# First stage's norms and casts re-ordered on their engine queues, the merge cut into five tiles of 410 columns, the last block finished by halves

## The chip, the cores and the metric

One Trainium2 chip; the same program runs on 8 cores with different data, without exchange between them. The time of a run is the device time of the slowest core, in microseconds (us). Engines: PE multiplies matrices, DVE and POOL work on vectors, ACT evaluates functions (and squares, scales, copies), SP issues most of the DMAs. Each engine works through its own queue in program order and waits there on semaphores.

## The reference, cut to what matters

```python
h = rmsnorm(x, norm_mix_pre)                     # x / rms(x) * w
q_m, k_m, v_m, i_m, f_m, o_m, q_f, k_f, v_f, f_f, g_a, g_b = split(h @ w_in)
h_a = mlstm_chunkwise(q_m, k_m, v_m, log_i, log_f)      # 4 heads, matrix memory
h_a = rmsnorm(h_a, ml_head_norm) * sigmoid(o_m)
y_a = h_a @ w_branch_a
h_b = forgetting_attention(q_f, k_f, v_f, log_fg)       # 8 heads, causal softmax
y_b = h_b @ w_branch_b
merged = sigmoid(g_a + b_gate_a) * y_a + sigmoid(g_b + b_gate_b) * y_b
x = x + rmsnorm(merged @ w_out, norm_mix_post)
h = rmsnorm(x, norm_ffn_pre)
a, g = split(causal_dwconv(h @ w_up, conv_w, conv_b))
x = x + rmsnorm((gelu(g) * a) @ w_down, norm_ffn_post)
```

x is (4, 4096, 1024); two cores share a batch row, each computes 2048 output tokens.

## The kernel before, in words

A core sees 32 blocks of 128 tokens. Blocks 0 to 14 (and 8 of them for the other half of the row) are only read for state and keys; blocks 15 to 31, 17 in number, are its own (block 15 gives a halo of two tokens). Nothing schedules the program: the Python code appends operations to five queues, a dependency tracker turns reads and writes of named buffers into semaphore waits, and each queue runs in the order in which it was written.

**Stage B (the mLSTM, 0 to about 412 us).** Each block of x is loaded, squared and summed on ACT (`A_sq`), turned into 1/rms (`rms_rstd`: a small multiply-add on DVE, then a power on POOL), scaled to bf16 on DVE (`A_sc`), transposed on PE and copied from PSUM on DVE (`A_T`). Blocks 0 to 7 are done first, in a lead-in loop that also runs the K projection of a block (`K_proj`, evacuated on ACT) and the gate columns (`A_G`). Every eight blocks the gates go through `gates_slot` (DVE add, ACT tanh), `gates_slot_b` (DVE, ACT exp), `gates_slot_c` (ACT ln, DVE negate into LF) and `gates_slot2` (two PE matmuls of LF, then small ACT and DVE work). Then one step for each chunk `c` in the order MSEQ (0 to 14, 16 to 23, 15, 24 to 31), `cn` being the next one: projections of `cn` (`QK_proj` of up to four blocks when `cn` opens a tile, `V_proj` in two halves, `O_proj` in two halves), state update `upd`, output `num_mm`, its norm (`num_post`: four ACT squares, small DVE work, a POOL power) and product (`num_fin` on DVE), and the store of the result `hablk` to memory (`T_ha`, on SP). `ctb` scales the state to bf16 on ACT for the next `num_mm`; `state_step` mixes states at three places. The projections take two PSUM banks in turn, so a projection waits until the one before the last is evacuated by ACT. `hablk` and the banks of `num_mm` are each reused: `hablk` every second chunk, and before this change `num_post` wrote its unused squares into `hablk` too. Weights arrive in f32 in twelve pieces and are cast to bf16 by `W_cast`, the last six at fixed places in `A_sc`, on POOL. From step 15 on, every step also issues one 1 MB conversion of `w_up` from POOL's queue (`conv_job`), whose DMA shares the 16 DMA engines with the stores.

**Stage C (attention, to about 966 us)** is not touched. **Stage D1, the merge (966 to 1194 us):** for each of 8 output column chunks and each token tile, four groups of 8 matmuls into four PSUM banks, two sigmoids on ACT, two products on DVE, a sum on POOL into `mergedT`. The tiles are 2 columns (the halo) and four times 512. The weights of the next chunk are cast (`wd_cast`: POOL and DVE) during the chunk. **Stage D2 and E** are the output projection and the FFN, in four tiles of four blocks; at the end of a tile each block's down projection is squared on ACT, normed, added (POOL) and stored.

```python
        def rms_rstd(col, inv_n):      # dve tensor_scalar, then pool pow
        def A_sq(b):                   # act Square + rms_rstd(b)
        def A_sc(b):                   # dve scale; W_cast(LOAD_AT[b - 4]); W_load; A_load
        def num_post(c):               # 4 act squares, dve, pool pow
        def num_fin(c, p):             # dve: hablk = bank * scale * gate
```

## Time and profile before

| | us |
|---|---|
| median of 3 runs | 1733.96 (1731.91 to 1738.88) |
| the profiled execution | 1734.73 |
| its span, slowest core (4) | 1733.2 |
| spans of all cores | 1714.6 (core 7) to 1733.2 |
| PE busy on core 4 | 1637.2 (94%) |

The span is measured from the first to the last instruction of a core; the time has 1.5 us more around it. All sums below are made on core 4's trace. In the timelines a row has the start, the duration (of several merged instructions, from the first start to the last end), engine, line, operation, shapes and count, and in brackets how long the engine stood idle before and what ended the wait. Matmuls are pipelined, so a single one shows a latency that is longer than its share of a series.

### The profile page before, as it was taken

The page shows a single profiled execution, that of the slowest core. Times are in us where ns is not written, and L with a number is a line of the kernel's source. Part 1 is how long each engine was busy: PE and PEld are TensorE (multiplying, and loading weights), DVE is VectorE, ACT ScalarE, POOL GpSimd, SP SyncE. Part 2 cuts the span into 40 slices and gives each one's busy share as a digit, 9 for nine tenths or more (in the row PEclk, how much of TensorE's full clock was granted, in tenths as well). Part 3 has the DMA queues.
Part 4 walks back from the last instruction along what each step waited for, and adds up shares of the span by engine and source line. Part 5 has one row for each costly group of instructions (what it writes and reads, how often), then busy time and mean ns, then how long its engine had stood idle before and what let it go on. Part 6 is the DMA issues. An engine that isn't in the chain of part 4 may idle for free.

```text
span 1733.2 us, 36312 instructions; the slowest of 8 cores (1714.6 to 1733.2 us)
## 1 busy us (share of the span) xinstructions
PE 1637.2 (94%) x12448; PEld 915.4 (53%) x12448; DVE 833.5 (48%) x1599; ACT 904.9 (52%) x1709; POOL 447.6 (26%) x564
## 2 busy tenths in 40 slices
PE   3789996999999999999998999999999999999997
PEld 2345543455776776776775444444454444444443
DVE  4574644455334334333343223232887387584781
ACT  3455654555477677677678422122665164362551
POOL 1031111101111111111112223232843343343442
PEclk9899998999999999999999999999999999999999
DMA  9261368533632231331222522215684353443421
GB/s 296 94 222 62 68 82 119 69 56 62 102 37 27 30 40 23 32 48 23 32 35 59 113 89 69 78 50 155 180 252 138 76 183 95 136 161 81 146 98 49
DMA packets 102083, 163.23 MB, mean 94 GB/s; under 512 B 72848, under 2 KB 75152, under 8 KB 92688
## 3 DMA queue, kind: packets, MB, share of 16 engines
q1 hardware_dynamic: 78432, 134.50, 26.6%
q0 software_dynamic: 23040, 25.69, 12.9%
q8 instruction: 104, 1.70, 0.4%
q10 hardware_dynamic: 432, 0.72, 0.2%
q14 instruction: 75, 0.61, 0.1%
HBM read 160.63 MB, written 30.15 MB: 110 GB/s over the span
## 4 chain that ended last, share of the span: by engine, by line
PE 81%; DVE 5%; ACT 5%; issue 3%; DMA 3%; POOL 2%; SPq 0%; DVEq 0%; POOLq 0%; ACTq 0%
PE psum L381 51%; PE psum L1084 10%; PE psum L1638 6%; PE psum L1228 6%; PE psum L1561 5%; ACT arena L1208 2%; DVE arena L520 1%; ACT arena L528 1%; DMA ha_scr<-arena 1%; DMA arena<-x 1%; DMA arena<-wup_scr 1%; PE psum L505 1%; POOL arena L1665 1%; DVE arena L1419 1%; PE psum L818 1%
## 5 line engine op out<-in xcount | busy, mean ns | idle before, releaser
L381 PE MATMUL psum<-arena 128*128 128x512 bf16 (+2 forms) x6796 | 1138.2, 313 | 39.8 <-ACT arena L528 16.5
L381 PEld LDWEIGHTS psum<-arena 128*128 128x128 bf16 x6796 | 548.2, 99 | 490.6 <-issue 74.2
L1208 ACT ACTIVATE arena<-psum,arena 128x512 bf16<-128x512 f32 (+1 forms) x576 | 370.9, 651 | 144.4 <-PE psum L381 132.1
L1594 DVE SCALAR_TENSOR_TENSOR arena<-psum,arena 128x511 f32<-128x511 f32 x352 | 255.1, 746 | 48.5 <-POOL arena L1583 19.6
L1061 DVE CAST arena<-psum 128x512 bf16<-128x512 f32 (+3 forms) x164 | 104.2, 642 | 246.9 <-PE psum L1084 133.5
L1084 PE MATMUL psum<-arena 128*128 128x512 bf16 (+3 forms) x896 | 219.2, 348 | 3.5 <-DVE arena L1061 2.6
L1228 PE MATMUL psum<-arena 128*128 128x129 bf16 x2112 | 214.0, 220 | 1.5 <-POOL arena L1213 1.2
L1228 PEld LDWEIGHTS psum<-arena 128*128 128x128 bf16 x2112 | 155.3, 98 | 70.2 <-issue 2.8
L1638 PE MATMUL psum<-arena 128*128 128x512 bf16 x704 | 153.1, 379 | 1.5 <-POOL arena L1609 1.3
L1577 ACT ACTIVATE arena<-psum,arena 128x512 f32<-128x512 f32 x176 | 135.6, 778 | 23.2 <-PE psum L381 20.9
L1213 POOL TENSOR_TENSOR arena<-arena 128x128 bf16<-128x128 bf16 x128 | 59.1, 469 | 336.6 <-ACT arena L1208 334.9
L1609 POOL TENSOR_TENSOR arena<-arena 128x512 bf16<-128x512 f32 x88 | 112.9, 1283 | 110.1 <-ACT arena L1606 97.8
L351 POOL TENSOR_TENSOR arena<-arena 128x1 f32<-128x1 f32 x82 | 50.4, 620 | 278.1 <-DVE arena L348 278.1
L1638 PEld LDWEIGHTS psum<-arena 128*128 128x128 bf16 x704 | 68.6, 98 | 85.2 <-issue 2.9
L520 DVE SCALAR_TENSOR_TENSOR arena<-arena,psum 128x256 f32<-128x256 f32 (+1 forms) x188 | 81.2, 476 | 64.9 <-PE psum L1228 46.1
L1084 PEld LDWEIGHTS psum<-arena 128*128 128x128 bf16 x896 | 80.2, 98 | 56.6 <-issue 6.7
L1357 ACT ACTIVATE arena<-psum,arena 128x512 f32<-128x512 f32 (+1 forms) x40 | 24.0, 601 | 140.2 <-PE psum L381 140.1
L528 ACT ACTIVATE arena<-psum 128x512 bf16<-128x512 f32 (+3 forms) x93 | 51.3, 556 | 84.2 <-PE psum L381 83.8
L1363 DVE TENSOR_TENSOR arena<-psum,arena 128x512 f32<-128x512 f32 (+1 forms) x40 | 23.4, 585 | 133.9 <-ACT arena L1357 118.1
L528 ACT ACTIVATE arena<-psum,arena 128x256 bf16<-128x256 f32 x128 | 53.3, 467 | 60.9 <-PE psum L381 60.4
L1561 PE MATMUL psum<-arena 128*128 128x512 bf16 x352 | 85.0, 376 | 0.0
L1369 POOL TENSOR_TENSOR arena<-arena 128x512 bf16<-128x512 f32 (+1 forms) x40 | 44.3, 1107 | 155.9 <-DVE arena L1366 155.8
(114 smaller groups left out, 1222.8 us busy)
## 6 DMA issues: line engine op xcount, KB each, us to landing
arena<-wup_scr SPq DMA_DIRECT2D x44, 1024.0 KB, 5.8
arena<-x SPq DMA_DIRECT2D x33, 512.0 KB, 5.9
arena<-w_merge SPq DMA_DIRECT2D x32, 512.0 KB, 6.2
arena<-w_mem SPq DMA_DIRECT2D x12, 1024.0 KB, 10.9
wup_scr<-w_up POOLq DMA_DIRECT2D x11, 1024.0 KB, 15.1
arena<-x SPq DMA_DIRECT2D x8, 1024.0 KB, 8.0
out<-arena SPq DMA_DIRECT2D x16, 512.0 KB, 2.9
arena<-w_fox POOLq DMA_DIRECT2D x24, 256.0 KB, 4.8
```

Source lines behind the costliest of these rows:

```text
L381: ins = e.matmul(out_ap, lhsT=l, rhs=r, start=(i == 0), stop=(i == n - 1))
L520: pg.add("dve", lambda e: e.scalar_tensor_tensor(out=o, in0=a, scalar=sc_, in1=b_, op0=op0, op1=op1), reads=rd, writes=wr)
L528: pg.add("act", lambda e: e.activation(out=o, in_=a, func=func, scale=scale, bias=bias), reads=rd, writes=wr)
L1061: pg.add("dve", lambda e: e.tensor_copy(out=out_ap, in_=in_ap), reads=rd, writes=wr)
L1084: ins = e.matmul(bank(bk)[:, 0:w_], lhsT=Wqk.ap[:, kc, which * P:(which + 1) * P], rhs=tv[:, kc, :], start=(kc == 0), stop=(kc == KC - 1))
L1208: pg.add("act", lambda e: e.activation(out=pt.ap[:, c0:512], in_=bank(lgb)[:, 0:512 - c0], func=AF.Exp, scale=float(P) ** -0.5, bias=bias_ ...
L1228: ins = e.matmul(bank(ACC[tl % 2][i // 2])[:, (i % 2) * 129:(i % 2) * 129 + 129], lhsT=pt.ap[:, i * P:(i + 1) * P], rhs=vx[s_].ap[:, j, :] ...
L1561: e.matmul(bank(bk)[:, 0:w_], lhsT=l, rhs=r, start=(kc == 0), stop=(kc == KC - 1))
L1577: pg.add("act", lambda e, ups=ups, yb=yb, cidx=cidx, ag=ag, w_=w_: e.activation(out=yb.ap[:, ag, 0:w_], in_=ups[:, 0:w_], func=AF.Identity ...
L1594: pg.add("dve", lambda e, ups=ups, yb=yb, cidx=cidx, sh=sh, jw=jw, ag=ag, w_=w_: e.scalar_tensor_tensor(out=yb.ap[:, ag, sh:w_], in0=ups[: ...
L1609: pg.add("pool", lambda e, yb=yb, gl=gl, fi=fi, w_=w_: e.tensor_tensor(out=actb.ap[:, fi, 0:w_], in0=gl.ap[:, 0:w_], in1=yb.ap[:, 0, 0:w_] ...
L1638: ins = e.matmul(bank(bs[hh]), lhsT=actb.ap[:, fc, bl * P:(bl + 1) * P], rhs=Wdn(fc)[:, hh * 512:(hh + 1) * 512], start=(fc == 0), stop=(f ...
```

## The change

Six things. (1) `rms_rstd` leaves `A_sq`: it is queued, and emitted by `A_rstd`, at fixed places or at the latest in front of the `A_sc` that needs it. (2) The twelve weight casts alternate between ACT and DVE, none is on POOL; the loads of the last six, and so their casts, come earlier. (3) In the lead-in the K projection runs one block earlier, and the casts 2 to 5 are moved. (4) In the chunk loop `gates_slot_c` comes right behind `num_mm`, `ctb` and `state_step` go behind the second V projection, and `gates_slot2` behind the first O projection (for own chunks); `num_post` writes its unused squares into the scratch `jk`. (5) The merge runs in five tiles of 410 columns that begin at the halo's two columns. (6) The last block of the last tile is squared, scaled, added and stored in two halves of 512 columns, the first sum on POOL, the second on DVE.

```diff
         PIECES = [(ch, hf) for ch in (1, 2, 3, 0, 4, 5) for hf in range(2)]
-        CAST_ENG = ("act", "dve", "act", "dve", "pool", "dve") + ("pool",) * 6
-        LOAD_AT = {b: j for j, b in enumerate(range(12, 18), 6)}
+        CAST_ENG = ("act", "dve") * 6
+        LOAD_AT = {b: j for j, b in enumerate((10, 12, 14, 16, 17, 19), 6)}
...
+        sqq = []
         def A_sq(b):
...
-            rms_rstd(b, 1.0 / D)
+            sqq.append(b)
+
+        def A_rstd():
+            while sqq:
+                rms_rstd(sqq.pop(0), 1.0 / D)
         def A_sc(b):
...
+            if b in sqq:
+                A_rstd()
...
             def num_post(c):
-                hb_, gw = hablk[par], Gw[par]
+                gw = Gw[par]
                 for h in range(4):
                     pg.add("act", lambda e, h=h: e.activation(
-                        out=hb_.ap[:, h * 256:(h + 1) * 256], in_=bank(RB[h // 2])[:, h % 2 * 256:h % 2 * 256 + 256],
+                        out=jk.ap[:, h * 256:(h + 1) * 256], in_=bank(RB[h // 2])[:, h % 2 * 256:h % 2 * 256 + 256],
                         func=AF.Square, scale=eb_t.ap[:, c, h:h + 1], accum_out=sc.ap[:, par, 0, h:h + 1]),
-                        reads=[bank_u[RB[h // 2]], (eb_t.u, c // 8)], writes=[(sc.u, (par, "q")), (hb_.u, h)])
+                        reads=[bank_u[RB[h // 2]], (eb_t.u, c // 8)], writes=[(sc.u, (par, "q")), (jk.u, h)])
...
             A_sq(1)
             A_sc(1)
             A_sq(2)
+            pg.add("dve", lambda e: e.tensor_copy(out=Wg.ap, in_=Wgf.ap), reads=[Wgf], writes=[Wg])
+            K_proj(0)
             A_T(1)
-            pg.add("dve", lambda e: e.tensor_copy(out=Wg.ap, in_=Wgf.ap), reads=[Wgf], writes=[Wg])
+            A_G(0)
             for b in range(2, 8):
                 A_sc(b)
                 if b < 7:
                     A_sq(b + 1)
                 A_T(b)
-                K_proj(b - 2)
-                A_G(b - 2)
-            W_cast(2)
-            A_G(6)
+                if b < 7:
+                    K_proj(b - 1)
+                A_G(b - 1)
+                if b == 6:
+                    W_cast(2)
             A_G(7)
             gates_slot(0)
+            W_cast(3)
             gates_slot_b()
-            W_cast(3)
             gates_slot_c()
+            W_cast(5)
             W_cast(4)
             for b in range(8, 12):
                 A_load(b)
             gates_slot2(0, SB1)
             V_proj(0, 0)
-            W_cast(5)
             V_proj(1, 0)
             A_sq(8)
             A_sc(8)
                 if own(c):
                     gs = G_all()
                     num_mm(c)
+                    if late is not None:
+                        gates_slot_c()
                     if fresh or not own(cn):
...
                         gates_slot_c()
+                    A_rstd()
...
                     k_trans(cn)
                     if own(c) and not fresh:
                         num_post(c)
+                    A_rstd()
                 if cn is not None and (own(cn) or cn > 5):
                     V_proj(cn, 0)
                 if own(c) and cn is not None:
                     upd(c, 0)
                     upd(c, 1)
-                    if cn in (15, 24):
-                        state_step(cn)
-                    elif own(cn):
-                        ctb(cn, 0)
-                        ctb(cn, 1)
                 if own(c):
                     num_fin(c, 0)
                     num_fin(c, 1)
-                if late is not None and own(c):
-                    gates_slot_c()
                 if gs is not None:
                     gates_slot(gs)
                 if tails:
                     A_T(tails[0])
                 if cn is not None:
                     V_proj(cn, 1)
-                if late is not None:
-                    gates_slot2(late, TB if own(cn) else SB1)
+                if own(c) and cn is not None:
+                    if cn in (15, 24):
+                        state_step(cn)
+                    elif own(cn):
+                        ctb(cn, 0)
+                        ctb(cn, 1)
+                if late is not None and not own(cn):
+                    gates_slot2(late, SB1)
                 if gs is not None:
                     gates_slot_b()
                 gs2 = gs
...
                 if own(cn):
                     O_proj(cn, 0)
+                if late is not None and own(cn):
+                    gates_slot2(late, TB)
...
+            MT0, MTW = P - 2, 410
             for cc in range(KC):
                 wd = Wd[cc % 2]
                 wd_load(cc + 1)
-                for (eb0, nb_) in EXT_TILES:
-                    w_ = nb_ * P if eb0 else 2
-                    t0 = eb0 * P if eb0 else P - 2
+                for dt in range(5):
+                    t0, w_ = MT0 + dt * MTW, MTW
                     bs = [0, 1, 2, 3] if dstep % 2 == 0 else [4, 5, 6, 7]
                     dstep += 1
                     srcs = (haT, hbT, xnT_own, xnT_own)
...
                         if src is xnT_own:
-                            rd = [(src.u, NPRE + eb0 + j) for j in range(nb_)]
+                            rd = [(src.u, NPRE + j) for j in range(t0 // P, (t0 + w_ - 1) // P + 1)]
                         elif src is haT:
                             rd = [haT]
                         else:
-                            rd = [(src.u, (h, eb0 if eb0 else "E")) for h in range(8)]
+                            rd = [(src.u, (h, e0 if e0 else "E")) for h in range(8) for (e0, n0) in EXT_TILES
+                                  if e0 * P < t0 + w_ and (e0 + n0) * P > t0]
...
-                    if eb0 == 9:
+                        reads=[m1, m2], writes=[(mergedT.u, (cc, dt))])
+                    if dt == 3:
                         wd_cast(cc + 1)
...
-                                 bank_u[p0 + hh], [(mergedT.u, (kc, tile_eb[eb])) for kc in range(KC)] + [(Wout.u, hh)])
+                                 bank_u[p0 + hh], [(mergedT.u, (kc, dt)) for kc in range(KC) for dt in range(5)
+                                  if MT0 + dt * MTW < (eb + 1) * P and MT0 + (dt + 1) * MTW > eb * P] + [(Wout.u, hh)])
...
+                    elif last and ib == 3:
+                        for hh in range(2):
+                            e3_mm(bl, hh, bs, 0, NFC)
+                            pg.add("act", lambda e, hh=hh, bs=bs, tme=tme: e.activation(
+                                out=tme.ap[:, hh * 512:hh * 512 + 512], in_=bank(bs[hh]), func=AF.Square,
+                                accum_out=ssq.ap[:, 90 + hh:91 + hh]),
+                                reads=[bank_u[bs[hh]]], writes=[(ssq.u, 90 + hh), (tme.u, hh)])
+                        tt(ssq.ap[:, 90:91], ssq.ap[:, 90:91], ssq.ap[:, 91:92], ALU.add, [(ssq.u, 90), (ssq.u, 91)], [(ssq.u, 90)])
+                        rms_rstd(90, 1.0 / D)
+                        for hh, eng_ in ((0, "pool"), (1, "dve")):
+                            sl, xk = slice(hh * 512, hh * 512 + 512), (x1.u, eb) if hh else (x1.u, (eb, 0))
+                            stt(tme.ap[:, sl], bank(bs[hh]), rstd.ap[:, 90:91], wfpost_bc.ap[:, sl], ALU.mult, ALU.mult,
+                                [bank_u[bs[hh]], (rstd.u, 90), wfpost_bc], [(tme.u, hh)])
+                            pg.add(eng_, lambda e, eb=eb, tme=tme, sl=sl: e.tensor_tensor(
+                                out=x1.ap[:, eb, sl], in0=x1.ap[:, eb, sl], in1=tme.ap[:, sl], op=ALU.add),
+                                reads=[(tme.u, hh), xk], writes=[xk])
+                            pg.add("sp", lambda e, eb=eb, sl=sl: e.dma_start(out=out_d[(eb - 1) * P:eb * P, sl], in_=x1.ap[:, eb, sl]),
+                                   reads=[xk], writes=[(out_u, "o%d_%d" % (eb, hh))], dma="outh%d" % hh)
+                        continue
...
```

How the order on two queues moves. DVE in the lead-in, from the scaling of block 2 (SCALAR_TENSOR_TENSOR 128x1024 is `A_sc`, TENSOR_SCALAR 128x1 the DVE half of `rms_rstd`, COPY the one in `A_T`), before:

```order
L486 SCALAR_TENSOR_TENSOR arena<-arena 128x1024
L348 TENSOR_SCALAR arena<-arena 128x1
L508 COPY arena<-psum 128x8x128
L486 SCALAR_TENSOR_TENSOR arena<-arena 128x1024
L348 TENSOR_SCALAR arena<-arena 128x1
```

and now:

```order
L494 SCALAR_TENSOR_TENSOR arena<-arena 128x1024
L516 COPY arena<-psum 128x8x128
L348 TENSOR_SCALAR arena<-arena 128x1
L494 SCALAR_TENSOR_TENSOR arena<-arena 128x1024
L516 COPY arena<-psum 128x8x128
```

The norm's DVE half went from in front of the copy to behind it, directly in front of the scaling that needs its result.

ACT in the steps of chunks 22 and 23 (128x256 from psum,arena is half a V projection's evacuation or, at L780/L788, a square of `num_post`; 128x256 from arena is `ctb`; 128x64 is tanh, the 128x96 are exp and then ln of the gates; 128x512 is an O projection's tanh; 128x128 x8 evacuates the Q and K of block 15), before:

```order
L780 ACTIVATE arena<-psum,arena 128x256 x4
L528 ACTIVATE arena<-psum,arena 128x256 x2
L528 ACTIVATE arena<-arena 128x256 x4
L528 ACTIVATE arena<-arena 128x64
L528 ACTIVATE arena<-psum,arena 128x256 x2
L528 ACTIVATE arena<-arena 128x96
L528 ACTIVATE arena<-psum 128x512 x2
L780 ACTIVATE arena<-psum,arena 128x256 x4
L528 ACTIVATE arena<-psum 128x128 x8
L528 ACTIVATE arena<-psum,arena 128x256 x2
L528 ACTIVATE arena<-arena 128x256 x4
L528 ACTIVATE arena<-arena 128x96
```

and now:

```order
L788 ACTIVATE arena<-psum,arena 128x256 x4
L536 ACTIVATE arena<-psum,arena 128x256 x2
L536 ACTIVATE arena<-arena 128x64
L536 ACTIVATE arena<-psum,arena 128x256 x2
L536 ACTIVATE arena<-arena 128x256 x4
L536 ACTIVATE arena<-arena 128x96
L536 ACTIVATE arena<-psum 128x512 x2
L536 ACTIVATE arena<-arena 128x96
L788 ACTIVATE arena<-psum,arena 128x256 x4
L536 ACTIVATE arena<-psum 128x128 x8
L536 ACTIVATE arena<-psum,arena 128x256 x4
L536 ACTIVATE arena<-arena 128x256 x4
```

`ctb` went behind the second V evacuation, and the gates' ln in front of the squares.

PE between the second V projection of block 15 and its `num_mm` (128x96 are the two LF matmuls of `gates_slot2`, the 128x512 a V projection and then two O projections, or V and O and then O), before:

```order
L381 MATMUL psum<-arena 128x512 x8
L381 MATMUL psum<-arena 128x96 x2
L381 MATMUL psum<-arena 128x512 x16
L761 MATMUL psum<-arena 128x256
L762 MATMUL psum<-arena 128x256
```

and now:

```order
L381 MATMUL psum<-arena 128x512 x16
L381 MATMUL psum<-arena 128x96 x2
L381 MATMUL psum<-arena 128x512 x8
L769 MATMUL psum<-arena 128x256
L770 MATMUL psum<-arena 128x256
```

One O projection now stands in front of the LF matmuls.

## Rows read from the trace of the kernel before

**Rows 1.** The page: span, and busy time of the engines.

```profile
span 1733.2 us, 36312 instructions; the slowest of 8 cores (1714.6 to 1733.2 us)
...
PE 1637.2 (94%) x12448; PEld 915.4 (53%) x12448; DVE 833.5 (48%) x1599; ACT 904.9 (52%) x1709; POOL 447.6 (26%) x564
```

**Rows 2.** Timeline, lead-in: start, us, engine line operation [idle before <-what ended it].

```profile
35.38 1.28 DVE L486 SCALAR_TENSOR_TENSOR arena<-arena 128x1024 bf16<-128x1024 f32 x1 [0.63 <-POOL arena L351]
...
36.81 0.61 PE L505 MATMUL psum<-arena 128*128 128x128 bf16 x8 [1.01 <-DVE arena L486]
...
37.46 0.15 DVE L348 TENSOR_SCALAR arena<-arena 128x1 f32<-128x1 f32 x1 [0.79 <-ACT arena L478]
...
37.56 0.69 DVE L508 COPY arena<-psum 128x1024 bf16<-128x1024 bf16 x1
...
38.48 1.28 DVE L486 SCALAR_TENSOR_TENSOR arena<-arena 128x1024 bf16<-128x1024 f32 x1 [0.22 <-POOL arena L351]
...
42.00 2.75 DVE L486 SCALAR_TENSOR_TENSOR arena<-arena 128x1024 bf16<-128x1024 f32 x1 [0.22 <-POOL arena L351]
...
47.82 1.90 ACT L465 ACTIVATE arena<-arena 128x2048 bf16<-128x2048 f32 x1
...
52.73 7.52 PE L381 MATMUL psum<-arena 128*128 128x96 f32 x24 [4.91 <-DVE arena L524]
```

**Rows 3.** Timeline of core 4, chunks 19 and 22.

```profile
222.77 0.47 ACT L780 ACTIVATE arena<-psum,arena 128x256 bf16<-128x256 f32 x1 [4.04 <-PE psum L381]
...
225.93 11.97 PE L381 MATMUL psum<-arena 128*128 128x512 bf16 x51 [3.17 <-ACT arena L528]
...
267.69 1.89 PE L381 MATMUL psum<-arena 128*128 128x512 bf16 x8
...
272.35 0.47 ACT L780 ACTIVATE arena<-psum,arena 128x256 bf16<-128x256 f32 x1 [5.52 <-DMA ha_scr<-arena]
...
275.76 3.02 PE L381 MATMUL psum<-arena 128*128 128x512 bf16 x8 [3.91 <-ACT arena L528]
...
280.79 3.57 PE L381 MATMUL psum<-arena 128*128 128x512 bf16 x8 [2.01 <-ACT arena L528]
```

**Rows 4.** DMA issues, 250 to 256 us: line, queue, count, KB, us to landing.

```profile
ha_scr<-arena SPq DMA_DIRECT2D x1, 256.0 KB, 17.2
```

**Rows 5.** Timeline of core 4: QK_proj(16), the LF matmuls, O_proj(24).

```profile
168.99 10.52 PE L381 MATMUL psum<-arena 128*128 128x512 bf16 x48 [1.87 <-ACT arena L528]
...
302.56 6.32 PE L381 MATMUL psum<-arena 128*128 128x96 f32 x20 [6.10 <-DVE arena L524]
...
332.98 1.89 PE L381 MATMUL psum<-arena 128*128 128x512 bf16 x8 [2.21 <-ACT arena L528]
```

**Rows 6.** Timeline of core 7: QK_proj(16) and the LF matmuls.

```profile
164.46 10.52 PE L381 MATMUL psum<-arena 128*128 128x512 bf16 x48 [1.87 <-ACT arena L528]
...
286.14 5.77 PE L381 MATMUL psum<-arena 128*128 128x96 f32 x20 [6.10 <-DVE arena L524]
```

**Rows 7.** Timeline of core 4, before the LF matmuls: ACT.

```profile
298.80 1.71 ACT L528 ACTIVATE arena<-arena 128x256 bf16<-128x256 f32 x4 [3.67 <-DVE arena L517]
...
300.52 1.28 ACT L528 ACT_TABLE_LOAD   x1
```

**Rows 8.** Windows of PE over the merge: from:to, length, busy (count), clock, DMA, GB/s.

```profile
966.37:1194.50 228.13, 227.77 (x1280) 1.00 0.31 79
```

**Rows 9.** Timeline: POOL in the merge.

```profile
990.10 1.58 POOL L1369 TENSOR_TENSOR arena<-arena 128x512 bf16<-128x512 f32 x1 [5.64 <-DVE arena L1366]
...
991.64 2.34 POOL L1291 TENSOR_TENSOR arena<-arena 128x1024 bf16<-128x1024 f32 x1
```

**Rows 10.** Timeline, the end of the program.

```profile
1715.80 8.15 PE L1638 MATMUL psum<-arena 128*128 128x512 bf16 x37
...
1724.16 1.02 ACT L1658 ACTIVATE arena<-psum 128x1024 f32<-128x1024 f32 x1 [8.38 <-PE psum L1638]
...
1727.75 2.34 POOL L1665 TENSOR_TENSOR arena<-arena 128x1024 f32<-128x1024 f32 x1 [1.53 <-DVE arena L1662]
```

More of the change, by code:

```diff
@@ L1370, in build_program @@
                         out=mergedT.ap[:, cc, t0:t0 + w_], in0=m1.ap[:, 0:w_], in1=m2.ap[:, 0:w_], op=ALU.add),
-                        reads=[m1, m2], writes=[(mergedT.u, (cc, eb0))])
-                    if eb0 == 9:
+                        reads=[m1, m2], writes=[(mergedT.u, (cc, dt))])
+                    if dt == 3:
                         wd_cast(cc + 1)
@@ L1432, in build_program @@
                 load_group(k_)
-            tile_eb = {}
-            for (eb0, nb_) in EXT_TILES:
-                for j in range(nb_):
-                    tile_eb[eb0 + j] = eb0
             for n in range(NEXT + 3):
```

## The prediction, made before the change was run

> **What bounds the kernel now.** I read the page first. PE is busy 94% of the span [rows 1], so only two things can shorten the run: fewer PE cycles, or less waiting of PE. The windows by stage then showed that almost all of PE's idle time lies before 340 us, in stage B; the merge is full, so there only fewer cycles help. The waits of PE led to the timeline of stage B, where four kinds of wait stand out.
> The lead-in [rows 2]: a scaling (35.38), transposes (36.81), a copy (37.56), the next scaling (38.48), 3.1 to 3.5 us a block. One scaling took 2.75 us instead of 1.28, because a cast ran on POOL beside it, and PE then stood 4.91 us before the first LF matmuls at 52.73.
> Chunks 19 and 22 [rows 3]: ACT stands 4.04 and 5.52 us before the squares of `num_post`. The second is put down to the store `ha_scr`; that store took 17.2 us to land [rows 4], and 272.35 less 17.2 is its issue, about 255.1. The first is put down to PE, which had long been done; the square writes the same buffer that the store reads, so I take it for the same wait. Behind the squares stands the evacuation of a V projection, and PE waits 3.17, 3.91 and 2.01 us for it. After the waits eight matmuls take 3.02 and 3.57 us instead of the 1.89 at 267.69: PE is then for a while at the lower of its two levels (1.2 instead of 2.4 GHz), so a wait costs more than its own length.
> A check inside this trace: core 7 has none of these store waits, and its span is the 1714.6 us of [rows 1]. From the first Q/K projection (168.99 and 164.46) to the LF matmuls of the last eight blocks (302.56 and 286.14) core 4 needs 133.6 us and core 7 121.7 [rows 5, 6].
> Last, the LF matmuls at 302.56, with 6.10 us of idle PE on both cores [rows 5, 6].
>
> **The change, term by term** (core 4's trace; the profiled execution took 1734.7 us, 0.8 above the median of the runs).
>
> *Lead-in: -1.4.* The norm's DVE half now stands behind the copy, so the chain of a block is serial: 1.43 (scaling to transposes) + 0.75 (to the copy) + 0.69 - 0.1 (overlap) + 1.02 (norm half at 37.46 to the scaling at 38.48) = 3.8 us against 3.3 before, five times: +2.5. The POOL cast beside block 7 is gone: 2.75 - 1.28 = -1.5. The ACT cast of 1.90 at 47.82, which stood in front of the tanh, has moved into the loop, where ACT idles: -1.9. The last K projection no longer stands in front of the last gate matmuls (1.7 us, from eight matmuls in 1.89), but a DVE cast now does in front of `gates_slot_b` (1.2): -0.5. Ends: -4 (the chain hides behind PE) and +2.5 (only the chain shows).
>
> *Chunk loop, blocks 8 to 23: 0.* The six casts leave POOL for ACT (1.90 each, [rows 2]) and DVE. On DVE a scaling and a cast (about 2.5 us) take the place of a scaling of 2.8 that a POOL cast slows. Where a step has two new blocks, the norm half adds up to 1.0 us to DVE's chain. ACT has room beside PE. Both signs: -3 to +3. `A_rstd` in the other steps stands where its result is needed a projection later: nothing.
>
> *Squares into jk: -11.9.* They no longer wait for a store. I take the difference of the two cores, 133.6 - 121.7. What then remains is what core 7 has. `num_fin` still overwrites the stored buffer, but a good 5 us later in the step (about 17.5 us after the store's issue against 12.3), and 17.2 was the slowest store. POOL's queue also issues one 1 MB conversion earlier, in a stretch in which the DMA engines idled. Ends: -13 and -5.
>
> *Chunk 23 to block 24's Q and K: -1.8.* E is the end of chunk 23's last O projection, 280.79 + 3.57 = 284.36. Before: LF matmuls at E + 18.2, `num_mm(15)` at E + 24.5 (302.56 + 6.32), the third Q/K group of block 24 at about E + 29.0 (1.0 for num_mm and two groups of 1.73). Now `num_mm(15)` waits for `ctb` alone: it began at E + 14.4 [rows 7]; ln and its table load come in front of the squares (+1.5), `num_fin` in front of `state_step` (+1.7), so it ends at 14.4 + 3.2 + 1.7 = E + 19.3. But ACT then has everything in a row: table load 1.28, two tanh and the gate operations (about 3.2, sized from 1.71 for the four operations of 256 columns of `ctb`), squares and first evacuation (3.4, from 272.35 to 275.76): third group at E + 27.2. So 5 us come free, and 3.4 are given back to ACT's queue. Ends: -6 and +2.
> The table load took 1.28 us in this trace, and started 0.01 us after the work before it (298.80 + 1.71 = 300.51, [rows 7]). The Trainium skill (ScalarE: Activation LUTs, What ACT_TABLE_LOAD costs) adds a drain and gives about 2.66 us for every switch of a set. With that the two loads on this path would cost some 2.8 us more and the term would be +1.0; the row shows no such gap, so the sum goes by the row.
>
> *State step of block 24: -0.7.* PE waited 2.21 us for a V evacuation that stood behind `ctb` [rows 5]. The evacuation is now in front, but the next `num_mm` waits for a `ctb` that is 1.7 later.
>
> *The merge: -5.9.* Eight matmuls of 512 columns took 1.89 us [rows 3], eight of 128 columns 0.61 [rows 2]: 1.28 / 8 / 384 = 0.417 ns a column. 48 of 512 columns took 10.52 [rows 5], so one more costs (10.52 - 1.89) / 40 = 215.8 ns, and one of 410 columns 215.8 - 102 x 0.417 = 173.3. Before: 1024 of 512 columns and 256 of two, 228.1 in all and 227.8 of them busy [rows 8], which leaves about 28 ns for a two-column one. Now 1280 x 173.3 + 0.4 (idle) = 222.2. Same columns, but 256 instructions of 28 ns fewer and a little more fixed cost. Ends: -6.9 (pure proportion to columns) and 0 (a straight line between 2 and 512 columns, 178.2 ns). Evacuations shrink with the columns and stay hidden. POOL's cast of the next weights ended (991.64 + 2.34) about 1.1 us before its chunk did [rows 9]; with the last tile at 5.5 instead of 6.9 us this cover is down to about 0.1. If it is gone, some 0.3 us are added seven times.
>
> *The end: -1.6.* PE stopped at 1723.95; square 1.02, norm 1.1, scaling 1.3, sum 2.34, DMA 3.1 to 1733.2 [rows 10]. By halves: last half's square 0.6, an addition 0.2, norm 1.1, two half scalings 1.3, one half sum 0.7 (DVE; POOL's runs beside it), 0.3 for a second DMA: 4.5 with starts against 6.1.
>
> Sum: -1.4 - 11.9 - 1.8 - 0.7 - 5.9 - 1.6 = -23.3; 1734.7 - 23.3 = 1711.4, or 1711 against the median.
>
> **The rivals.**
> *The store wait only changes its place.* `num_fin` is now the first to need the buffer; if a store lands 3 us late, DVE stands with the state updates' followers behind it. For it: the stores share DMA engines with conversions. Against: core 7, and the later need. Half of the term comes back: 1717. Chance 0.14.
> *DVE's chain.* The lead-in shows all of its +2.5, and double blocks 1 us each, four times, instead of my -1.4 and 0: 1719. Chance 0.06.
> *The 410 columns bring nothing* (178 ns each): 1717. Chance 0.05.
> *The drain of table loads* shows, by the rule above: 1714. Chance 0.03.
> *More than forecast.* ACT catches up behind block 15, so that the 5 us stay, and the lead-in's chain hides: 1705. Chance 0.12.
> *Slower.* The store lands so late that `num_fin` holds `num_mm`'s banks: `num_mm` of the next chunk overwrites what `num_fin` reads, so PE stops at once, in all of chunks 18 to 23, and the steps, now packed closer, push the conversions closer too. The slack is 17.5 us plus some 1.6. It turns slower than before by over 0.5% from 1743, which is 32 us over the forecast, 5.3 in each of six chunks: stores landing 24 us after issue, where 17.2 was the worst. Chance 0.05.
>
> **How the numbers follow.** The forecast has 0.55. A measurement of this kernel tells 0.5% (8.7 us, 1725.3) from no change. Faster by more: forecast, both 1717, 1719, 1714 and 1705 less 0.05 for several of them together: 0.90. Within: that 0.05 and 0.01 of the slower case: 0.06. Slower: 0.04. The range takes in 1705 with some of the larger end of the block-15 term, and the 1717 to 1719 cases with their spread: 1702 to 1723.
>
> **What would show it.** Right: no ACT wait for `ha_scr` before L788; core 7 and core 4 within a few us of each other; in the merge eight matmuls of 410 columns pitch 173 ns and the stage takes 222 us; LF matmuls without the 6 us wait, but a wait of PE for ACT in block 24's Q/K groups; scalings 3.8 us apart in the lead-in; from PE's last matmul to the end 7.7 us instead of 9.3. Wrong: DVE waiting for `ha_scr` at `num_fin`; PE waiting for POOL's weight cast in the merge; idle stretches in the steps of blocks 9 to 23 longer than now, with 512-column matmuls at half rate behind them.

## The result, and the profile after

The change took **1723.16 us** (median of five executions) against 1733.96 before: a ratio of 0.9935, 95% interval 0.9911 to 0.9959. It is faster, by 10.8 us (11.3 by the ratio) where 23 were forecast, and lies just outside the range that ended at 1723. One of the five took 1944.04 us with the cores of one die at a granted clock of 0.84 to 0.85; such executions, which the kernel before has too, are left out of the ratios and of all medians further down (without it the change's four run from 1722.25 to 1723.17).

The page's span and busy time, beside [rows 1]:

```profile
span 1720.7 us, 36342 instructions; the slowest of 8 cores (1704.4 to 1720.7 us)
...
PE 1627.5 (95%) x12448; PEld 932.6 (54%) x12448; DVE 828.3 (48%) x1605; ACT 909.4 (53%) x1715; POOL 432.1 (25%) x557
```

The spans of its cores (first to last instruction, and the mean granted clock) are the first thing to read:

```profile
core 0: 1705.0 us, clock 0.990
...
core 2: 1720.7 us, clock 0.988
core 3: 1704.4 us, clock 0.993
core 4: 1717.9 us, clock 0.987
...
core 6: 1717.8 us, clock 0.990
```

Cores 0 and 3 are where the forecast put all of them, and even a little lower. Cores 2, 4 and 6 are 13 to 16 us behind. The time is that of the slowest core, so the question is what core 2 does that core 3 does not. From the change's waits between 150 and 345 us (engine and line, what it waited for: us in total, times, longest), core 2:

```profile
DVE arena L528 <- DMA ha_scr<-arena: 13.4, 1, 13.4
...
PE psum L381 <- DVE arena L525: 12.2, 1, 12.2
```

Core 3 has neither line; on cores 4, 5 and 6 DVE waits 9.4, 3.6 and 9.9 us in the same way, on cores 0, 1 and 7 not at all. L528 is the scaling in `num_fin`, which overwrites the buffer that `T_ha` stored two chunks before. The timelines of core 2 (start, us, engine, line, operation, idle before) place it; DVE, and then PE:

```profile
224.03 1.66 DVE L528 SCALAR_TENSOR_TENSOR arena<-psum,arena 128x256 bf16<-128x256 f32 x4 [13.37 <-DMA ha_scr<-arena]
```

```profile
212.81 1.46 PE L381 MATMUL psum<-arena 128*128 128x512 bf16 x6
226.43 0.36 PE L381 MATMUL psum<-arena 128*128 128x16 bf16 x8 [12.16 <-DVE arena L525]
```

The wait is one, at chunk 18, earlier than the waits of [rows 3], and as long as two or three of them. The gate matmuls behind it (128x16) need the transposed block that DVE copies behind `num_fin`. Which store is it? DVE was released at 224, and the first store of all was issued at 196.50. The DMA issues of core 2 in three short windows give us from issue to landing: the first conversion (POOL, at 191.91), the last load of x (SP, at 196.08), the first store (SP, at 196.50).

```profile
wup_scr<-w_up POOLq DMA_DIRECT2D x1, 1024.0 KB, 16.1
arena<-x SPq DMA_DIRECT2D x1, 512.0 KB, 17.5
ha_scr<-arena SPq DMA_DIRECT2D x1, 256.0 KB, 27.4
```

The store took 27.4 us: 196.5 + 27.4 = 223.9. The second store, issued at 202.9, took 24.8 us, but the one wait had by then moved the step that needs its buffer behind its landing. Before, on the same core, the same first store took 5.0 us. What changed is the order of the issues. POOL of core 2, the change:

```profile
190.43 1.02 POOL L801 TENSOR_TENSOR arena<-arena 128x4 f32<-128x4 f32 x1 [10.27 <-DVE arena L348]
191.42 0.55 POOL L351 TENSOR_TENSOR arena<-arena 128x1 f32<-128x1 f32 x1
191.91 0.76 POOL L850 DMA_DIRECT2D wup_scr<-w_up  x1
```

and POOL of core 2 in the kernel before, with SP of the same stretch under it:

```profile
190.45 1.02 POOL L793 TENSOR_TENSOR arena<-arena 128x4 f32<-128x4 f32 x1 [2.45 <-DVE arena L520]
196.81 0.55 POOL L351 TENSOR_TENSOR arena<-arena 128x1 f32<-128x1 f32 x1 [5.33 <-DVE arena L348]
197.31 0.76 POOL L842 DMA_DIRECT2D wup_scr<-w_up  x1
```

```profile
196.68 0.33 SPq L449 DMA_DIRECT2D arena<-x  x1
197.11 0.38 SPq L836 DMA_DIRECT2D ha_scr<-arena  x1
```

L351 is the small power of a block's norm. In front of the conversion in POOL's queue it was a brake: it waited for its square until 196.81, and so the first 1 MB conversion went out 0.2 us behind the first store. `A_rstd` emits that power one step later, when its square is long done. Between `num_post`'s power (L801) and the conversion POOL now waits for nothing, and the conversion goes out 4.6 us ahead of the store and 4.2 ahead of a load of x. All three then share the core's DMA engines. The eight cores issue the conversion 190.1 to 193.0 us after their own start; how far the starts lie apart, the traces do not say. The next conversion follows on core 2 at 200.63, 4.1 us behind the store.

The stages, as means over the eight cores of the profiled runs, in us, worked out from the first and the last row of each stage on each core (LF: first LF matmuls; QK16: first Q and K projection; C and E: stages behind the chunk loop, the merge between them):

| | first transposes to LF | LF to QK16 | QK16 to C | C | merge, with the end of C | E up to its last matmul | last matmul's start to end |
|---|---|---|---|---|---|---|---|
| before | 37.5 | 115.1 | 242.7 | 477.1 | 372.2 | 459.4 | 9.6 |
| change | 36.8 | 114.5 | 235.4 | 477.9 | 367.6 | 458.2 | 7.8 |

Differences named further down are those of the unrounded means. In the column QK16 to C core 3 of the change takes 229.9 us and core 2 takes 244.7; core 7 of before, the clean one, took 233.7. In column C, which the change does not touch, core 7 of the change takes 481.8 us where five others take 477.1 to 477.2. That is why it ends at 1710.4, though it waits for no store.

Rows that answer to [rows 5, 6], PE of core 3: the last O projection of chunk 23, the third Q/K group of block 15, `num_mm(15)`, block 24's Q and K, `num_mm(24)`:

```profile
266.03 1.89 PE L381 MATMUL psum<-arena 128*128 128x512 bf16 x8 [1.77 <-ACT arena L536]
...
272.94 4.81 PE L381 MATMUL psum<-arena 128*128 128x128 bf16 x51 [3.06 <-ACT arena L536]
...
287.86 0.27 PE L769 MATMUL psum<-arena 128*128 128x256 bf16 x1 [1.46 <-ACT arena L536]
...
290.57 15.62 PE L381 MATMUL psum<-arena 128*128 128x512 bf16 x67 [1.14 <-ACT arena L536]
...
315.66 0.27 PE L769 MATMUL psum<-arena 128*128 128x256 bf16 x1 [0.92 <-ACT arena L536]
```

The 6.10 us in front of the LF matmuls are gone. The four waits for ACT from 272.94 on (3.06, 1.46, 1.14 and 0.92) took their place (on core 7 of before the first of them was 1.47 us long), and the 2.21 of [rows 5] is not among them. The merge, [rows 8], core 2: its window, and the last long run of its matmuls:

```profile
962.63:1186.67 224.04, 223.16 (x1280) 1.00 0.25 80
```

```profile
1159.81 26.86 PE L381 MATMUL psum<-arena 128*128 128x410 bf16 x154
1187.17 3.18 PE L381 MATMUL psum<-arena 128*128 128x512 bf16 x14 [0.50 <-DVE arena L1380]
```

One matmul of 410 columns runs 0.34 us from start to end, so the pitch is (26.86 - 0.34) / 153 = 173.3 ns, the figure of the forecast. And the end, [rows 10], core 2:

```profile
1707.80 5.56 PE L1652 MATMUL psum<-arena 128*128 128x512 bf16 x25
...
1713.46 0.60 ACT L1668 ACTIVATE arena<-psum 128x512 f32<-128x512 f32 x1 [2.67 <-PE psum L1652]
...
1716.36 1.26 POOL L1678 TENSOR_TENSOR arena<-arena 128x512 f32<-128x512 f32 x1 [1.00 <-DVE arena L528]
1716.98 1.19 DVE L1678 TENSOR_TENSOR arena<-arena 128x512 f32<-128x512 f32 x1
```

### The profile page after: what moved, and what is told of

Same layout as the page of the kernel before. It is cut to its first block, busy times and chain, and to the rows that moved or that the text cites. A ratio compares the mean times of both kernels' runs of the same rounds, so it can differ in the third digit from the quotient of the medians.

```text
span 1720.7 us, 36342 instructions; the slowest of 8 cores (1704.4 to 1720.7 us)
## 1 busy us (share of the span) xinstructions
PE 1627.5 (95%) x12448; PEld 932.6 (54%) x12448; DVE 828.3 (48%) x1605; ACT 909.4 (53%) x1715; POOL 432.1 (25%) x557
## 3 DMA queue, kind: packets, MB, share of 16 engines
q0 software_dynamic: 23040, 25.69, 10.4%
## 4 chain that ended last, share of the span: by engine, by line
PE 83%; DVE 4%; ACT 4%; issue 4%; DMA 3%; POOL 1%; DVEq 0%; ACTq 0%; SPq 0%; POOLq 0%
PE psum L381 51%; PE psum L1100 10%; PE psum L1652 9%; PE psum L1244 6%; PE psum L1575 5%; DVE arena L528 2%; ACT arena L1224 2%; DMA ha_scr<-arena 2%; ACT arena L536 1%; PE psum L513 1%; PE psum L826 1%; DMA arena<-norm_mix_pre 1%; DVE arena L494 1%; POOL arena L351 0%; DMA arena<-wup_scr 0%
## 5 line engine op out<-in xcount | busy, mean ns | idle before, releaser
L381 PE MATMUL psum<-arena 128*128 128x512 bf16 (+3 forms) x6796 | 1128.8, 313 | 42.1 <-ACT arena L536 12.2
L381 PEld LDWEIGHTS psum<-arena 128*128 128x128 bf16 x6796 | 566.0, 99 | 465.2 <-issue 70.8
L1224 ACT ACTIVATE arena<-psum,arena 128x512 bf16<-128x512 f32 (+1 forms) x576 | 371.2, 651 | 143.8 <-PE psum L381 132.3
L1100 PE MATMUL psum<-arena 128*128 128x512 bf16 (+3 forms) x896 | 219.2, 348 | 3.7 <-DVE arena L1077 2.6
L1244 PEld LDWEIGHTS psum<-arena 128*128 128x128 bf16 x2112 | 155.4, 98 | 70.1 <-issue 2.6
L351 POOL TENSOR_TENSOR arena<-arena 128x1 f32<-128x1 f32 x82 | 50.0, 615 | 258.9 <-DVE arena L348 258.9
L1652 PEld LDWEIGHTS psum<-arena 128*128 128x128 bf16 x704 | 68.6, 98 | 84.0 <-issue 1.7
L528 DVE SCALAR_TENSOR_TENSOR arena<-arena,psum 128x256 f32<-128x256 f32 (+1 forms) x188 | 81.3, 477 | 65.2 <-PE psum L1244 46.4
L1100 PEld LDWEIGHTS psum<-arena 128*128 128x128 bf16 x896 | 80.3, 98 | 56.8 <-issue 6.8
L1374 ACT ACTIVATE arena<-psum,arena 128x410 f32<-128x410 f32 x40 | 24.1, 603 | 139.7 <-PE psum L381 139.6
L1380 DVE TENSOR_TENSOR arena<-psum,arena 128x410 f32<-128x410 f32 x40 | 23.4, 585 | 133.8 <-ACT arena L1374 125.8
L1386 POOL TENSOR_TENSOR arena<-arena 128x410 bf16<-128x410 f32 x40 | 44.2, 1105 | 151.8 <-DVE arena L1383 151.7
```

The source lines that it names most:

```text
L381: ins = e.matmul(out_ap, lhsT=l, rhs=r, start=(i == 0), stop=(i == n - 1))
L528: pg.add("dve", lambda e: e.scalar_tensor_tensor(out=o, in0=a, scalar=sc_, in1=b_, op0=op0, op1=op1), reads=rd, writes=wr)
L1100: ins = e.matmul(bank(bk)[:, 0:w_], lhsT=Wqk.ap[:, kc, which * P:(which + 1) * P], rhs=tv[:, kc, :], start=(kc == 0), stop=(kc == KC - 1))
L1224: pg.add("act", lambda e: e.activation(out=pt.ap[:, c0:512], in_=bank(lgb)[:, 0:512 - c0], func=AF.Exp, scale=float(P) ** -0.5, bias=bias_ ...
L1244: ins = e.matmul(bank(ACC[tl % 2][i // 2])[:, (i % 2) * 129:(i % 2) * 129 + 129], lhsT=pt.ap[:, i * P:(i + 1) * P], rhs=vx[s_].ap[:, j, :] ...
L1652: ins = e.matmul(bank(bs[hh]), lhsT=actb.ap[:, fc, bl * P:(bl + 1) * P], rhs=Wdn(fc)[:, hh * 512:(hh + 1) * 512], start=(fc == 0), stop=(f ...
```

## The experiments

Theory A: the moved norm lets POOL issue the first conversion ahead of the first store, and the store lands too late. Theory B: the wait of the squares went to `num_fin` by itself. Theory C: the conversions crowd the memory in any order. Each run was timed beside the kernel before on its chip; ratios are to that.

**The norm's second half back in its old place, in the chunk loop.**

```
             sqq.append(b)
+            if b > 9:
+                A_rstd()
```

> The change, with the norm's second half (DVE and POOL) put back behind its square for the blocks of the chunk loop. In the change's trace POOL issues the first 1 MB conversion at 191.9 us, 4.2 us ahead of the last load of x (196.1) and 4.6 ahead of the first store of ha_scr (196.5); that store took 27.4 us to land and DVE stood 13.4 us for it at num_fin, PE 12.2. In the trace before, the conversion was issued at 197.3, 0.2 us behind the store. Theory A (the moved norm lets POOL run ahead, so the store queues behind the conversion and a load that is behind it too): the conversion comes behind the store again, the 13.4 us wait of DVE is gone, slow cores gain 8 to 12 us, time 1709 to 1713. Theory B (the wait of the squares has only moved to num_fin, whatever the order of the issues): DVE still waits some 9 to 13 us, time 1720 to 1724. Theory C (the eight cores' conversions crowd the memory and the order is of no account): as B.

Measured: 1710.87 us (1707.53 to 1715.00), ratio 0.9876 (0.983 to 0.9922). The conversion is behind the store again (core 5: store at 194.42, conversion at 194.76), and the first store lands in 4.6 to 6.0 us on every core. In the profiled execution no span is over 1708.7, and the longest wait for a store is 2.1 us, on core 5:

```profile
194.25 0.55 POOL L351 TENSOR_TENSOR arena<-arena 128x1 f32<-128x1 f32 x1 [4.84 <-DVE arena L348]
194.76 0.76 POOL L852 DMA_DIRECT2D wup_scr<-w_up  x1
```

```profile
who waited for it (us, times):
  DVE arena L530: 2.1, 1
...
DMA to landing us min/median/max: 2.0/8.9/19.6
```

That is A's number; B and C asked for 1720 to 1724. What nobody had expected: QK16 starts 2.6 us earlier behind LF (mean 111.9 us against 114.5). The moved norm had cost time in the loop too.

**Three buffers.** `hablk2` in the unused space behind `hablk1`; `num_fin` and `T_ha` take `hablk[MPOS[c] % 3]`.

```
-        cw("pad", [D], BF16)
+        hablk.append(cw("hablk2", [D], BF16))
...
-                hb_, gw = hablk[par], Gw[par]
+                hb_, gw = hablk[MPOS[c] % 3], Gw[par]
```

> The change, with three buffers hablk instead of two, so that num_fin needs the store of three chunks ago and not of two (some 10 us more slack for the first stores). Theories A, B and C alike: the store still takes 24 to 28 us on the slow cores, issued at about 196.5, and lands at about 224; the third num_fin that needs its buffer comes at about 221 instead of 211, so that 2 to 4 us of the 13.4 remain at most, and the slow cores end within 6 us of the fast ones: 1707 to 1712. If the wait were not what costs the slow cores their 13 us (another cause of the difference between the cores): 1720 to 1724.

Measured: 1711.95 us, ratio 0.9879 (0.9849 to 0.991), spans 1704.8 to 1711.5. On four cores the first store still takes 17.8 to 24.4 us, nearly as long as in the change (core 0, all stores between 185 and 330 us):

```profile
DMA to landing us min/median/max: 2.1/11.0/24.6
```

and nothing in the loop waits for them. So it is the wait that costs, not the traffic beside which the matmuls run.

**Conversions one step later.** `conv_job` is held in a list and emitted in front of the next step's V projection.

```
-                if 15 <= ip < 15 + NG:
-                    conv_job(ip - 15)
+                cq = [ip - 15] if 15 <= ip < 15 + NG else []
...
+                while cq:
+                    conv_job(cq.pop())
                 if cn is not None and (own(cn) or cn > 5):
                     V_proj(cn, 0)
```

> The change, with every conversion issued one step later on POOL, behind the small power of the next chunk, which puts the first one at about 200.6 us instead of 191.9, 4 us behind the first store. Theory A: the first store lands in under 10 us, no wait of DVE for it on any core, time 1706 to 1711. Theories B and C: the same number of conversions in the same stretch, only 9 us later, so the wait comes with a later store: 1718 to 1724.

Measured: 1712.69 us, ratio 0.9882 (0.9851 to 0.9914), spans 1704.4 to 1711.7; that is 1.7 us over A's range and 5 under that of B and C. No wait for a store in the loop; the first store lands in 4.2 to 5.0 us, the slowest of all after 11.6. The same eleven conversions, 9 us later: C is out as well, and A holds, as far as the order of the issues goes.

**Squares back in hablk, the rest as in the change** (`out=jk.ap` becomes `out=hb_.ap` again in `num_post`).

> The change, with the squares of num_post back in hablk. What the squares into jk bring by themselves: by the prediction 11.9 us, so 1735. Theory A: with the late store (landing at 224) the squares, which come some 5 us ahead of num_fin, wait for it as well, and for later stores too: 1726 to 1732. Theory B: the wait has only moved, so it is as long as in the change: 1722 to 1726.

Measured: 1722.68 us, ratio 0.9942 (0.9924 to 0.996): the time of the change. That was B's number, not A's. ACT waits for the same late store, core 5:

```profile
ACT arena L788 <- DMA ha_scr<-arena: 12.1, 1, 12.1
```

The first store lands when it lands; whether the squares or `num_fin` stands in front of it, PE stops until then, and on this core the one wait pushes the later steps back so far that they wait for no other store. In the change the squares in jk are worth nothing that these runs can tell.

**Squares in jk alone, in the kernel before.**

> The kernel before with one edit: the squares of num_post go into jk. POOL's order is the old one, so the first conversion comes 0.2 us behind the first store. By the prediction's term it gains 11.9 us: 1722. Theory A (a wait for a store costs by how late the store lands; who reads first matters only for a landing that falls between the squares and num_fin, some 5 us apart; with the old order the slow landings were 15 to 17 us, and num_fin comes about 17.5 us behind the store): most of the waits of ACT vanish and DVE waits 0 to 2 us, so the slow cores come down to the clean ones: 1718 to 1723. Theory B (the wait only moves to num_fin whatever the order): 1730 to 1734.

Measured: 1722.37 us, ratio 0.9938 (0.992 to 0.9956): by the ratio -10.7 us by itself, near the term of the prediction (-11.9). The longest wait for a store is 1.5 us (core 0: 2.7 us in two). So B is wrong as a rule: with the conversion behind the store the wait does not move. The order alone is not all of it, though: on core 0 the first store took 15.9 us with the conversion 0.2 us behind it, against 4.3 to 7.2 on the other seven.

**The conversion ahead, in the kernel before** (`conv_job` in front of `A_sq`, no other edit).

> The kernel before with one edit: POOL issues each conversion ahead of the norm's power instead of behind it, which puts the first one at about 192 us, some 5 us ahead of the first store, as in the change. The squares stay in hablk. Theory A: the first store now takes 20 to 28 us on the slow cores, the squares of chunk 18 wait some 10 to 14 us for it (none of before's waits was over 6); later waits shrink, as later stores have fallen behind their conversions' ends: time 1731 to 1742, and the longest wait for ha_scr over 9 us. Theories B and C (the order of the issues is of no account): waits and time as before, 1733 plus or minus 2, longest landing about 17 us.

Measured: 1732.70 us, ratio 0.9999 (0.9984 to 1.0013). The mechanism is there (core 1: conversion at 190.81, store at 196.49, issue to landing, and ACT's waits):

```profile
ha_scr<-arena SPq DMA_DIRECT2D x1, 256.0 KB, 20.3
```

```profile
ACT arena L780 <- DMA ha_scr<-arena: 11.4, 1, 11.4
```

Four cores (1, 3, 5, 7) wait 7.6 to 11.4 us once, the other four 0.2 to 3.3 us and end at 1715 to 1723. Before, on core 2, it was two waits:

```profile
ACT arena L780 <- DMA ha_scr<-arena: 11.1, 2, 5.7
```

The sum of these waits on the slow cores is the same (11.4 against 11.1), so the order alone costs nothing where the squares wait anyway. It costs some 10 us (the change against the first three runs, by the ratios) only where it brings back a wait that jk had removed. The time was inside A's range, but it fits B and C too; the landing and the longest wait are what tells them apart.

**Both remedies together:** norm back in the loop, and three buffers.

> The change with both remedies: the norm's second half back behind its square in the chunk loop, and three buffers hablk. Theory A: no wait for ha_scr on DVE or ACT is left on any core, and the 2 us by which the first Q and K projection starts earlier with the old norm order (163.2 us on the mean of five cores against 165.2) stay: all cores between 1701 and 1708, time 1706 to 1710. If the earlier start were only an accident of that run: 1711 to 1713, as with either remedy alone.

Measured: 1708.91 us, ratio 0.986 (0.9842 to 0.9878), spans 1702.0 to 1707.0, no wait for a store in the loop on any core. QK16 starts at 162.6 on the mean of eight cores, against 165.2 in the change: the 2.6 us come back in a second run.

**The same, with the ln of the gates behind the squares** (`gates_slot_c` and `num_post` exchanged).

> The kernel of the run with both remedies and one edit more: at the step of chunk 15 the ln of the gates and its table load stand behind the squares of chunk 23 on ACT and not in front. In the change's trace the third group of Q and K of block 15 waits 3.06 us for ACT, behind that table load (1.28) and the squares. If ACT's queue there is what PE waits for: that wait falls to 1.5 us or less, but the ln ends 2 us later, num_mm(15) waits up to 1 us more, and block 24's groups are as late as before: 0 to 2 us gained, 1705 to 1709. If DVE's chain of gate operations behind the ln is on the path instead: 1 to 3 us lost, 1709 to 1712.

Measured: 1709.87 us, ratio 0.9864 (0.9838 to 0.989), spans 1701.5 to 1708.3: no difference. The wait of 3.06 us is still 3.06: the exchange left the table load and the squares both in front of the evacuation that PE needs, so it could not tell what it was made for. To shorten the wait the ln has to go behind that evacuation; that was not tried.

**The merge alone,** in the kernel before.

> The kernel before with the merge alone changed, five tiles of 410 columns. Between the last matmul of the attention (L1084 or L1100) and the first evacuation of the next stage but one (L1577 or L1591) all cores of before take 371.2 to 372.8 us, those of the change 367.5 to 367.7, so 3.6 to 5.2 less. Theory: the term of the prediction, -5.9, and the time falls by 4 to 6: 1728 to 1730, with the stage waits for ha_scr as before. Rival (the stage is shorter but the gain goes elsewhere, because a later stage waits for loads that do not start earlier): under 2 us.

Measured: 1728.85 us, ratio 0.9967 (0.9954 to 0.998), so -5.7 by the ratio, with an interval of -8.0 to -3.5. The stage, with the end of C, took 367.3 or 367.4 us on every core against 371.2 to 372.8. The gain reached the end.

**The norm back in the lead-in too,** with three buffers (`A_rstd()` behind every `sqq.append(b)`).

> The kernel of the run with both remedies, with the norm's second half behind its square in the lead-in too. The prediction took the new lead-in as a serial chain of 3.8 us a block against 3.3 before, five times, +2.5 us; the change's trace shows 3.76 apart. If that chain is what PE waits for: scalings 3.1 to 3.5 apart, the first LF matmuls 1 to 2.5 us earlier after the first transposes (35.8 in the run with both remedies), time 1706.5 to 1708.5. If PE, slow at 1.2 GHz there, or POOL is the bound: same time, 1709.

Measured: **1706.15 us**, ratio 0.9839 (0.9823 to 0.9854), the fastest of all, slightly under the expectation. DVE of core 4, two scalings, and PE's LF matmuls:

```profile
38.49 1.28 DVE L495 SCALAR_TENSOR_TENSOR arena<-arena 128x1024 bf16<-128x1024 f32 x1 [0.23 <-POOL arena L351]
...
41.59 1.28 DVE L495 SCALAR_TENSOR_TENSOR arena<-arena 128x1024 bf16<-128x1024 f32 x1 [0.22 <-POOL arena L351]
```

The same pair in the change, core 2:

```profile
38.97 1.28 DVE L494 SCALAR_TENSOR_TENSOR arena<-arena 128x1024 bf16<-128x1024 f32 x1 [0.86 <-POOL arena L351]
...
42.73 1.28 DVE L494 SCALAR_TENSOR_TENSOR arena<-arena 128x1024 bf16<-128x1024 f32 x1 [0.86 <-POOL arena L351]
```

3.10 us apart instead of 3.76, and 33.0 us from the first transposes to LF on the mean of the cores, against 36.5 in the run with both remedies: the serial chain of the new norm order cost 3.5 us there.

## Why the prediction was wrong

It was wrong in one term, and that term in one sentence.

*Squares into jk, -11.9.* **The step that failed** is the bound beside it: "`num_fin` still overwrites the stored buffer, but a good 5 us later in the step (about 17.5 us after the store's issue against 12.3), and 17.2 was the slowest store." The 17.2 belonged to the old order of issues (and to core 4; core 2 of the same trace had a store of 18.6). The next sentence of the prediction saw the new one, "POOL's queue also issues one 1 MB conversion earlier", and closed it with "in a stretch in which the DMA engines idled". It idled only until 4 us later, when a load of x and the first store came. That store took 27.4 us, 10 more than the worst row that I had, and in place of the squares `num_fin` waited 13.4 us for it and PE 12.2. The term itself was about right for the edit alone (-10.7 measured) and worth nothing inside this change (ratio 0.9942 without it, 0.9935 with it). With a third buffer and no other edit the change takes 1711.95 us, where the forecast had 1711: the rest came out right in sum, partly by luck, since some of its parts cancel and two stages moved that it left out, as below.

*The rival "the store wait only changes its place"* is what came, at a chance of 0.14. I priced it at half of the term, 1717, by a store that is 3 us late. It was 10 us later than the worst row (13.4 us of wait), and the whole term went. The sign to look for, DVE waiting for `ha_scr` at `num_fin`, was the right one.

*Lead-in, -1.4:* first transposes to LF went from 37.5 to 36.8, -0.6. The chain cost +3.5 (I had +2.5), so the casts and the moved K projection together gave back about 4.1 (I had 3.9); that part has no run of its own.

*Chunk loop to block 16, 0:* LF to QK16 went from 115.1 to 114.5, -0.7. Again two parts that cancel: with the old norm order it is 111.9, so what else changed there, the casts off POOL above all, is worth -3.2, just outside the "-3 to +3" of the prediction, and `A_rstd` costs +2.6, where it said "nothing". That the -3.2 are the casts is argued and not tested. Which block pays the 2.6 was not looked into.

*Chunk 23 to block 24, and its state step, -1.8 - 0.7 = -2.5:* from `num_mm(23)` to `num_mm(24)` core 7 of before took 318.59 - 268.19 = 50.4 us and core 3 of the change 315.66 - 267.75 = 47.9. That is -2.5, the size of the forecast, and PE's waits for ACT show its mechanism: much of the freed time went back to ACT's queue. The state step's own figures, 2.21 less 1.7, give -0.5 and not the -0.7 of the sum; the two were not measured apart. The table load on ACT of core 3 started right behind its forerunner, without a gap:

```profile
286.81 1.71 ACT L536 ACTIVATE arena<-arena 128x256 bf16<-128x256 f32 x4 [3.34 <-DVE arena L525]
288.53 1.28 ACT L536 ACT_TABLE_LOAD   x1
289.83 0.82 ACT L536 ACTIVATE arena<-psum 128x512 f32<-128x512 f32 x2
```

(286.81 + 1.71 = 288.52.) By the Trainium skill (ScalarE: Activation LUTs, What ACT_TABLE_LOAD costs) a drain would stand there as well; this trace shows none, and the sum that went by the row was the right one.

*The merge, -5.9:* the stage with the end of C is 3.6 us shorter than on cores 4, 5 and 7 of before and 5.2 shorter than on the other five (on core 2 the granted clock of its first 10 us was 0.83, on core 4 it was 1.00, and the term was read from core 4); -5.7 by the ratio of the merge alone. The pitch of 173.3 ns was met. The stage is 224.0 us and not 222.2, against 228.1 on core 4 of before (-4.1): 1280 x 173.3 is 221.8, and 2.2 us come on top, 0.9 as stops of PE (0.36 at the first change of weights, 0.09 at each of the six others) and 1.3 within busy time. That is the size of the price that the forecast named and left out of the sum (0.3 us seven times, if POOL's cover is gone). Its cause stays open: the trace puts the 0.36 down to a product of DVE (L1380) that ended at 990.78, and POOL's weight cast ended at 990.64, so either could have held PE.

*The end, -1.6:* PE's last matmul ended at 1707.80 + 5.56 = 1713.36, 7.3 us before the end of the span, against 9.3. That is -1.9.

The columns E, -1.2 on the mean, and C, +0.8, were neither forecast nor followed up.

The two clean cores show what the terms come to without the late store: 1704.4 and 1705.0, against 1714.6 and 1718.5 for the two cores of before that waited least.

## What to carry to other kernels

An instruction that waits in a queue also holds back what stands behind it, and a transfer may owe its good place to that. When an edit shortens a wait on an engine that issues DMAs, list what the engine issues next, what else is issued in the following 10 us on other queues, and who needs the smallest of these transfers first. A landing time read from a trace is valid only for that order of issues: the same edit was worth 10.7 us alone and nothing beside another that made the transfer late. One more buffer took the cost of the late landing away here, without making the landing any earlier.

## What the hardware did that I had not expected

A 256 KB store that lands in 2.0 us at best took 27.4 when it was issued 4.6 us behind a 1 MB conversion, with a 512 KB load (17.5 us, 4.4 before) in between. It is not a fixed price: on core 3 of the same run, with the same order, the store landed in 8.7 us and the load in 8.3. In that run the cores that issued their conversion first, counted from their own start (0, 3 and 7, at 190.1 to 191.0 us), were all quick, and those that came later slow to different degrees (10.4 us on core 1, 27.4 on core 2). But with three buffers core 0 issued at 190.4 and its first store took 21.3, so the time from a core's own start does not decide it.

Four runs have the conversion ahead of the store: the change, three buffers, squares back, and conversion ahead in the kernel before. Of their 32 cores, 16 landed the first store in 6.0 to 12.1 us and 16 in 16.5 to 27.4, with nothing between. The first conversion itself took 8.4 to 13.2 us on the quick ones and 12.7 to 16.1 on the slow ones, so both are slow on the same cores, with some overlap. In all four runs the next conversion also follows 3.6 to 4.2 us behind the store and meets it in flight; with no conversion ahead that one did no harm (4.2 to 5.0 us, conversions one step later), but no run has the one ahead without the next. What makes one core slow and another quick, and why the small store suffers most, stays open.

The load and the store share SP's queue, and the store landed behind the load (196.08 + 17.5 = 213.6, then 223.9). The Trainium skill (DMA: Bandwidth & Descriptors, Queues, rings and completion order) has each DMA engine take turns between queues packet by packet and start the work of one queue in order; the trace agrees with that order on this core. It would explain a store behind the load and beside a conversion. It does not tell 27.4 us from the 8.7 of another core with the same queues.
